# A two-layer encoder step of split-precision products: a shorter warm-up, a hand-written third pair, a 16-column low-rank tile, rotary halves by DMA, a late fold and earlier output tiles

## The reference, cut to what matters

```
x += 1/2 * post(SwiGLU_1(pre(x)))                            # FFN 1, D_FF = 2816
x += post(W_out [GLA | DiffAttn | Retention](pre(x)))        # mixer: one W_in (1024 x 3344), one W_out
x += 1/2 * post(SwiGLU_2(pre(x)))                            # FFN 2
```

```
z = h @ w_in[l]                                  # its first 16 columns are a_lr
log_a = log_sigmoid(a_lr @ w_gla_a2[l] + b) / 16 # w_gla_a2 is (16, 128): the low-rank gate of GLA
q_r, k_r = rotary(rq), rotary(rk)                # per head of 64: [x1*cos - x2*sin, x1*sin + x2*cos]
p = softmax(q k^T - slopes * dist), masked       # two maps a head, for prompt and sample
o_d = (p[:, 0] - lam * p[:, 1]) @ v              # 4 heads, v of 128 columns
```

## Time and profile before

| | us |
|---|---|
| time, median of 3 runs | 1350.68 (1350.62 to 1351.5) |
| the profiled execution's own time | 1351.72 |
| its span | 1349.6, so 2.1 lie outside the span |

### The profile page before, as it was taken

One profiled execution on the slowest core, in us unless ns is written; L12 is line 12 of the kernel. 1 busy time (PEld: TensorE's weight loads), 2 busy tenths in 40 slices (PEclk: granted clock), 3 DMA queues, 4 the chain that ended last, 5 costly groups with the idle time before them and its releaser, 6 DMA issues.

```text
span 1349.6 us, 24688 instructions
## 1 busy us (share of the span) xinstructions
PE 1330.8 (99%) x9576; PEld 1300.6 (96%) x9576; DVE 821.7 (61%) x1257; ACT 637.0 (47%) x1011; POOL 132.7 (10%) x153
## 2 busy tenths in 40 slices
PE   8999999999999999999999999999999999999998
PEld 7999999998989999999999999999899999999998
DVE  6755543687766855554386555438876677565532
ACT  5444433654466644443464443437435575444333
POOL 1000000550000200000030000005600030000000
PEclk9999999999999999999999999999999999999999
DMA  7555565543344445555544544555333346555552
GB/s 203 170 168 159 161 167 150 157 128 82 96 119 126 124 143 154 147 141 152 152 121 145 155 144 144 152 152 160 96 96 86 98 125 172 146 149 151 145 144 66
DMA packets 351145, 187.16 MB, mean 139 GB/s; under 512 B 6608, under 2 KB 348396, under 8 KB 351080
## 3 DMA queue, kind: packets, MB, share of 16 engines
q1 hardware_dynamic: 347560, 177.37, 46.6%
q0 software_dynamic: 2736, 8.03, 1.8%
q10 hardware_dynamic: 784, 0.86, 0.2%
HBM read 181.90 MB, written 4.33 MB: 138 GB/s over the span
## 4 chain that ended last, share of the span: by engine, by line
PE 92%; DVE 4%; DVEq 1%; issue 1%; ACT 1%; DMA 1%; POOL 0%; ACTq 0%; SPq 0%; POOLq 0%
PE ps L678 28%; PE ps L679 27%; PE ps L680 27%; DVE w_l L546 1%; PE ps L987 1%; PE ps L915 1%; PE ps L738 1%; PE ps L890 1%; PE ps L1012 1%; PE ps L830 1%; PE ps L1025 1%; PE ps L731 0%; PE ps L1001 0%; PE ps L723 0%; DVE tiny L1623 0%
## 5 line engine op out<-in xcount | busy, mean ns | idle before, releaser
L678 PE MATMUL ps<-xn_l,w_h 128*128 128x320 f32 x1808 | 569.7, 315 | 1.2 <-DVE xn_l L1407 0.8
L679 PE MATMUL ps<-xn_h,w_l 128*128 128x320 f32 x1808 | 558.5, 309 | 0.0
L680 PE MATMUL ps<-xn_h,w_h 128*128 128x320 f32 x1808 | 558.4, 309 | 0.0
L546 DVE TENSOR_TENSOR w_l<-raw,w_h 128x1024 fp32r<-128x1024 f32 (+1 forms) x338 | 407.5, 1209 | 167.2 <-ACT w_h L537 166.7
L537 ACT ACTIVATE w_h<-raw 128x1024 fp32r<-128x1024 f32 (+1 forms) x338 | 348.4, 1035 | 216.5 <-DMA raw<-in_ffn_w_down_dram 124.9
L678 PEld LDWEIGHTS ps<-xn_l,w_h 128*128 128x128 f32 x1808 | 339.8, 188 | 6.8 <-DVE xn_l L1407 2.0
L679 PEld LDWEIGHTS ps<-xn_h,w_l 128*128 128x128 f32 x1808 | 339.9, 188 | 1.7
L680 PEld LDWEIGHTS ps<-xn_h,w_h 128*128 128x128 f32 x1808 | 339.7, 188 | 0.0
L678 PE MATMUL ps<-hid_l,w_h 128*128 128x320 f32 x704 | 217.5, 309 | 0.0
L680 PE MATMUL ps<-hid_h,w_h 128*128 128x320 f32 x704 | 217.4, 309 | 0.0
L679 PE MATMUL ps<-hid_h,w_l 128*128 128x320 f32 x704 | 217.4, 309 | 0.0
(11 more groups left out here) (270 smaller groups left out, 1208.3 us busy)
## 6 DMA issues: line engine op xcount, KB each, us to landing
raw<-in_ffn_w_up_dram SPq DMA_DIRECT2D x172, 512.0 KB, 3.8
raw<-in_ffn_w_down_dram SPq DMA_DIRECT2D x64, 448.0 KB, 3.7
raw<-in_w_in_dram SPq DMA_DIRECT2D x54, 512.0 KB, 3.8
raw<-in_ffn_w_down_dram SPq DMA_DIRECT2D x32, 512.0 KB, 3.9
raw<-in_w_out_dram SPq DMA_DIRECT2D x16, 512.0 KB, 4.1
const<-in_tables_dram POOLq DMA_DIRECT2D x8, 298.0 KB, 4.4
raw<-in_ffn_w_up_dram SPq DMA_DIRECT2D x8, 256.0 KB, 6.4
x_in<-in_x_prompt_dram SPq DMA_DIRECT2D x4, 256.0 KB, 6.2
```

Source lines behind the costliest of these rows:

```text
L546: dve.tensor_tensor(w_l[s][:, 0:cols], raw[s][:, 0:cols], w_h[s][:, 0:cols], ALU.subtract).then_inc(w_lo, 1)
L678: pe.matmul(out, w_h[s][:, w], xl, start=first, stop=False)
L679: pe.matmul(out, w_l[s][:, w], xh, start=False, stop=False)
L680: return pe.matmul(out, w_h[s][:, w], xh, start=False, stop=last)
```

## The change

It has five parts. Line numbers are those of the changed kernel, where they differ.

**1. The start.** The warm-up is 3 matmuls of 320 columns instead of 5 of 512. The first quarter of x_sample comes by the SP queue instead of ACT's. The third pair is written out in `first_opening`: for each unit the 8 products w_h·xn_h and 8 of w_h·xn_l, which wait for w_h alone, then 8 of w_l·xn_h; `stat_x` stands in the middle of the latter, and the transpose of `par_in` behind unit 4. ACT makes unit 4's w_h ahead of its last two squares.

```diff
-WARM = 5
+WARM = 3
...
+                if k == 0:
+                    sp.dma_start(x_in[64:128, 2, 0:2 * P], ins["x_sample"][0, :, 0:2 * P]).then_inc(x_chunk[0], 16)
...
-                    pe.matmul(ps[:, 3, :], sq_2[:, 0:P], sq_2[:, P:P + 512], start=True, stop=True)
+                    pe.matmul(ps[:, 3, 0:T], sq[0][:, 0:P], sq[0], start=True, stop=True)
...
-                pe.wait_ge(par_loaded, N_PAR)
-                pe.transpose(ps_m[:, 3, 0:ROWS], par_in[0:ROWS, :], C("ident")[0:ROWS, 0:ROWS]).then_inc(par_mm, 1)
+                for t in range(OPENING, OPENING + 2):
+                    def part(w, v, k0, k1, first=False, last=False):
+                        for k in range(k0, k1):
+                            mm = pe.matmul(ps[:, t, 0:T], w[:, k * P:(k + 1) * P], v[:, k, :], start=first and k == 0,
+                                           stop=last and k == KD - 1)
+                        return mm
+
+                    pe.wait_ge(w_hi, t + 1)
+                    part(w_h[t], xn_h, 0, KD, first=True)
+                    part(w_h[t], xn_l, 0, KD)
+                    pe.wait_ge(w_lo, t + 1)
+                    if t == OPENING:
+                        part(w_l[t], xn_h, 0, KD // 2)
+                        pe.wait_ge(first_consts, 16)
+                        stat_x(0, 0)
+                        part(w_l[t], xn_h, KD // 2, KD, last=True).then_inc(w_used, 1)
+                        pe.wait_ge(par_loaded, N_PAR)
+                        pe.transpose(ps_m[:, 3, 0:ROWS], par_in[0:ROWS, :], C("ident")[0:ROWS, 0:ROWS]).then_inc(par_mm, 1)
+                    else:
+                        part(w_l[t], xn_h, 0, KD, last=True).then_inc(w_used, 1)
 
...
+                    if l == 0 and n == 0 and k == KD - 1:
+                        hi(act, l, u0 + 4)
                     if k:
                         square(k - 1)
                 square(KD - 1)
-                for v in (4, 5):
+                for v in (5,) if l == 0 and n == 0 else (4, 5):
                     hi(act, l, u0 + v)
                 act.preload_act_table(ACT.Sqrt)
                 root_x(l, m)
```

```diff
+            sp.dma_start(a2[32:32 + RANK, :, :], ins["w_gla_a2"].rearrange("l r c -> r l c")).then_inc(lam_loaded, 16)
...
+            def low_rank_part(s, bank, k0, k1):
+
+                for k in range(k0, k1):
+                    w = w_h[s][:, k * P:(k + 1) * P]
+                    pe.matmul(ps[:, bank, 0:T], w, xn_l[:, k, :], start=k == 0, stop=False)
+                    mm = pe.matmul(ps[:, bank, 0:T], w, xn_h[:, k, :], start=False, stop=k == KD - 1)
+                if k1 == KD:
+                    mm.then_inc(w_used, 1)
```

```diff
             for l in range(DEPTH):
                 ffn(l, U_F1, ins["ffn1_w_up"], ins["ffn1_w_down"], 1 if l == 0 else 0)
-                for v in range(N_MIX):
-                    c = 0 if v == 0 else RANK + W_IN_TILE[v - 1] * P
+                sp.wait_ge(w_used, l * UNITS + U_MIX + 1)
+                sp.dma_start(low_rank(raw[slot(l, U_MIX)], 0), columns(ins["w_in"], l, slice(0, RANK))
+                             ).then_inc(raw_in[slot(l, U_MIX)], 16)
+                for v in range(1, N_MIX):
+                    c = RANK + W_IN_TILE[v - 1] * P
                     load(l, U_MIX + v, slot(l, U_MIX + v), columns(ins["w_in"], l, slice(c, c + P)), KD)
+                    n = v - RQ - 8
+                    if n in (0, 2):
+                        sp.wait_ge(evac, l * GROUPS + G_MIX + RQ + n + 3)
+                        for g in range(0, P, 32):
+                            sp.dma_start(y[g:g + 32, n:n + 2, :], z[g ^ 32:(g ^ 32) + 32, RQ + n:RQ + n + 2, :]
+                                         ).then_inc(turned_halves[n // 2], 16)
...
                 elif kind == "rot":
-                    zt, t = z[:, RQ + n, :], y[:, 7, :]
-                    after(dve, l, "pe", f"rot{n}")
-                    dve.drain()
-                    dve.tensor_tensor(t, ps[:, ROT_BANK[n], 0:T], C("sin"), ALU.mult)
+                    zt, t = z[:, RQ + n, :], y[:, n, :]
+                    dve.wait_ge(turned_halves[n // 2], (l + 1) * 64)
+                    dve.tensor_tensor(t, t, C("sin"), ALU.mult)
                     dve.tensor_tensor(zt, zt, C("cos"), ALU.mult)
                     dve.drain()
...
-("past", 1), ("rot", 0), ("weight", 0)] + P8[7][:1] + [("rot", 1), ("weight", 1)] + ... ("level", 2), ("rot", 2) ... ("level", 3), ("rot", 3)
+("past", 1), ("weight", 0)] + P8[7][:1] + [("weight", 1)] + ... ("level", 1), ("rot", 0) ... ("level", 2), ("rot", 1) ... ("level", 3), ("rot", 2) ... ("level", 4), ("rot", 3)
```

```diff
-                        if ATT[n][1] < 2:
-                            mm = pe.transpose(ps[:, 6, kt * P:(kt + 1) * P], p, C("ident"))
-                        else:
-                            mm = pe.matmul(ps[:, 6, kt * P:kt * P + T_S], p, C("fold"), start=True, stop=True)
+                        mm = pe.transpose(ps[:, 6, kt * P:(kt + 1) * P], p, C("ident"))
...
-                        o, w = (slice(b * P, (b + 1) * P), P) if b < 2 else (slice(T_P, T), T_S)
-                        mm = pe.matmul(ps[:, 7, o], v, probs_t[:, kt, 0:w], start=b == 0, stop=kt == b, skip_group_check=True)
+                        mm = pe.matmul(ps[:, 7, b * P:(b + 1) * P], v, probs_t[:, kt, :], start=b == 0, stop=kt == b, skip_group_check=True)
...
+                elif kind == "att_o":
+                    if n % 3 == 2:
+                        after(dve, l, "act", f"att_o{n}")
+                        v = y[:, 2 + n // 3, T_P:T]
+                        mark("dve", dve.tensor_tensor(v, v, ps[:, 7, T:T + T_S], ALU.add), f"att_o{n}")
...
+                    after(act, l, "dve", {"a": "att_o5", "b": "att_o8", "c": "att_o11"}[n])
```

```diff
+AHEAD_OUT = {3: (6,), 4: (7, 8), 5: (9, 10), 6: (11,)}
...
-                    if v < 5:
-                        hi(act, l, U_OUT + 6 + v)
-                    if v == N_OUT - 2:
-                        hi(act, l, U_F2 + 3)
+                    for u in AHEAD_OUT.get(v, ()):
+                        hi(act, l, U_OUT + u)
```

## The result

The changed kernel takes 1352.91 us (median of 20 runs, 1349.48 to 1355.24) where the kernel before takes 1350.61 (20 runs, 1348.13 to 1351.88). The ratio is 1.0019, with an interval of 1.0013 to 1.0025: slower by 0.2%, where a gain of 5.6 us was forecast. The profiled execution took 1352.82, with a span of 1351.0.

A forecast was written before the change was run, and what follows sets the result against it. PE was taken as the bound, busy 1330.8 of 1349.6 us. Low rank −1.6, rotary −3.9, fold −1.4, output tiles −0.1 and start +1.4 sum to −5.6, giving 1345.1, range 1341.3 to 1349.2.

The forecast's parts named there:

- the rotary: Mixer: removing PE's fp32 rotary products gives −4.3, new waits +0.2 a layer, so −3.9; bounds −0.5 and −6.3.
- the start: Opening: first product −1.0, later stat_x +0.6, lower clock +0.8 and +1.0, so +1.4; bounds −2.2 and +4.5.
- the replay of DVE's order: GLA levels: with old row durations, level 5's stall goes from 0.99 to 0.7 and level 7 gets 0.5.
- the lower bound: Rotary term: if DVE is the chain through the whole stretch, the four products bring nothing, about −0.5.
- The rival of the port: Rotary multiplication by sin, two SBUF inputs, port shared with GpSimd: 0.36 to 0.94 more each, about 1348.3; chance 0.17.
- The lower clock in the opening: First products after the shorter warm-up: up to 2.0 lost to half speed, 1.0 taken.
- The lower clock behind the pause: After PE's pause ahead of the fourth pair: up to 1.7 lost at the lower clock, 0.8 taken.
- the pause itself: PE's wait for w_l, moved behind the third pair, grows to some 3.4.
- Low rank: Low-rank unit: eight of 24 products go in each layer, 0.78 a layer after waits, −1.6; bounds −1.2 and −2.35.
- Fold: Before attention statistics: transposes replace products, −2.3, against +0.3 second product and +0.3 a layer waits: −1.4; bounds −2.3 and 0.
- Output tiles: Output tiles: same work in another order of splits, −0.1, between 0 and −0.3.
- the rival of the weight queue: SP's queue: loads of units 13 and 15 up to 2 us late behind the exchange; 1353.5 or above, chance 0.05.

The follow-up runs named there:

- run 4: Changed kernel with the rotary part undone (products on PE, old places and table, no exchange by DMA): 1351.70.
- Runs 7 and 12: 7: changed kernel with old start, rotary steps behind levels 4, 6, 7, 8, first keys' transposes later: 1343.16; 12: the same with rotary part undone: 1349.53.
- run 3: Kernel before, its rotary steps (products on PE, PSUM input) moved behind levels 1 to 4, all four products sharing one PSUM bank: 1363.99.
- Runs 1, 5 and 6: Changed kernel with, 1: whole old start, 1349.08; 5: only old warm-up and x_sample queue, 1351.06; 6: only old third pair, 1350.26.
- run 11: Kernel with old start, moved rotary steps and keys' transposes (1343.16), with the output tiles' splits in the old order: 1344.06.
- run 8: Kernel with old start, moved rotary steps and keys' transposes (1343.16), third pair written out again, DVE's parameter copies and lambda sums later: 1342.39.

## Why the prediction was wrong

**Direction and size.** It said 1345.1 in 1341.3 to 1349.2; it is 1352.91. Two terms failed, the rotary (predicted −3.9) and the start (+1.4); the median lies 7.8 above the forecast, and the two are off by 5.2 and 2.5.

**The rotary: the step that failed is the replay of DVE's order "with the durations of its rows".** It gave "level 5's stall becomes 0.7, and a new one comes at level 7"; measured are 1.2, 1.6 and 1.2 at levels 3, 4 and 5 and none at 7. PE's part was right (−1.08 where two products go, twice a layer). DVE's was not: a rotary step took 1.8 to 2.4 in the kernel before, and in the changed one three steps take 1.4 to 1.5 and step 0 takes 4.6, against a slack of 1.68 at its place. From there to level 5 the chain is DVE's: PE waited 0.99 for it at level 5 before and waits 3.9 at three levels now.

How much of this is step 0 alone is an estimate from the rows of layer 1, which no run tests: had it taken 1.45 like the others, the copy of level 2 could have begun at 959.76, as before, and not at 962.42, and the chain behind it would be 2.66 earlier. The stretch from level 0 to level 8 would then be 0.7 shorter than before, not 1.95 longer, and the part worth 1.8 a layer, close to the 1.96 of the prediction. Measured is the lower bound, "the four products are worth nothing if DVE is the chain through the whole stretch, about −0.5", and worse: the part costs 1.3 (0.7 a layer, run 4). Runs 7 and 12 show that the places of the steps decide: with the same DMAs and the same steps elsewhere, the part is worth 2.35 in layer 1.

**The rival of the port** has the right mechanism for one step in four, and that is the step that costs. The multiplication took 0.48 to 0.49 in six of eight cases, which its price of 0.36 to 0.94 more denies, and 1.85 and 1.86 in the two of step 0; the whole step took 4.6, against 2.3 at the same place with the PSUM operand (run 3). So the port is no rival of the place but a part of it: a place beside GpSimd's products is dear for a step with two SBUF operands. The Trainium skill ("SBUF — State Buffer", section "Who interferes with whom") has this as an exclusive lock on a port pair shared by DVE and GpSimd; the trace agrees for step 0 and shows three steps in four, with GpSimd idle during their multiplications, at the old duration. Overlap in the rows alone doesn't tell, though: in the kernel before, the multiplication by cos has two SBUF operands too and lies under rows of GpSimd in all eight cases, and it took 0.48 to 0.49 in six of them and 0.82 in two.

**The start: two terms of the sum mis-sized.** The first product came 0.63 earlier, not 1.0: the second transfer of x_prompt, now behind x_sample in SP's queue, is issued at 3.27 in place of 2.65 and lands at 9.0 in place of 8.6. Over all profiled executions even 0.63 is luck: the first product stood at 9.6 to 10.0 in the four with the short warm-up and at 9.7 to 10.7 in the ten with the long one, 0.3 apart on average. The lower clock in the opening cost 2.5 in the profiled execution, not 1.0 (and the bound given for it was 2.0), since it lasted from 8 to 15. It came in all four executions with the short warm-up, at a cost of 2.5, 1.1, 1.3 and 2.1, and in none of the ten with the long one. The lower clock behind the pause cost 1.4, not 0.8; the pause itself, 3.57, was predicted as 3.4. It came in three of the four executions with that pause. The sum sets it against a start that keeps its clock, as the execution of the kernel before that is shown does; but behind the old pause of 2.07 at `stat_x` the clock fell in seven of nine executions. `stat_x` came 0.7 later against the opening, predicted 0.6. Runs 1, 5 and 6 give 3.8 for the whole and 1.9 and 2.7 for the halves. The mechanism was right, and 3.95 lies within the prediction's upper bound of 4.5.

**The rest.** Low rank: predicted 0.78 a layer, measured 0.88 to 0.89. Fold: predicted 0.70, measured 0.61 to 0.62. Output tiles: predicted 0.1, no difference in the lap of layer 1 (run 11). The exchange by DMA landed in 2.3 to 3.8 us, and no queue behind it was late; the rival of the weight queue didn't come.

## What to carry to other kernels

Where PE already waits for an engine inside a stretch, that engine is close to being the chain of the stretch. Find the slack at each place in its own timeline; what a change adds to its queue beyond that slack is paid in full, and what it takes off PE there brings nothing. Price the added instructions by rows from the place where they will stand: a step of 1.4 us took 4.6 beside GpSimd's products. A mend that only moves a wait behind other work mends nothing; follow the late operand back to what is queued ahead of it (here DVE's copies of parameters ahead of a split). After a change, compare laps between like landmarks before medians, since they keep apart what the clock does and what the work costs.

## What the runs showed of the hardware

The granted clock falls to 0.50 for about 3.5 us at the few places where PE pauses or does small products only (`stat_x` at 28, the norms at 250, 436, 676 and 1098), in some executions and not in others. A lap over one FFN is 238.7 to 239.0 without such a drop and 239.8 to 240.2 with one, so a drop costs about 1.1. The profiled executions had from none to four of them between the opening and the last 5 us. This goes with the spread of a kernel: the changed one takes 1349.5 at a mean granted clock of 0.999 and 1355.2 at 0.992, and run 8, whose profile shows no drop before the last 5 us, takes 1342.0 to 1342.7 at 0.998 to 0.999. Behind the waits of 1.2 to 1.6 at the levels of the changed kernel the clock did not fall; in the mixers of run 3 it fell behind waits of 3.5 and 3.2, and not behind two of 2.0 and 2.1.

The multiplication by sin of 128x320 took 0.49 with one operand in PSUM in all 32 cases, beside GpSimd or not, and 0.47 to 1.86 with both in SBUF.
